# Hybrid decoder layer on Trainium2: a gate projection moved in front of the SSD scan's decay steps, and the sample group's SSD step rearranged

## The reference, cut to what matters

```
def step(h, inp):                       # one chunk
    xi, dti, dai, bi, ci = inp
    cum = jnp.cumsum(dai, axis=1)
    seg = cum[:, :, None] - cum[:, None, :]
    decay = jnp.exp(jnp.where(mask, seg, -jnp.inf))
    cb = jnp.einsum('bign,bjgn->bijg', ci, bi)
    m = cb[..., None] * decay * dti[:, None]
    y = jnp.einsum('bijgh,bjghp->bighp', m, xi)
    y = y + jnp.einsum('bign,bghpn->bighp', ci, h) * jnp.exp(cum)[..., None]
    last = cum[:, -1]
    w = jnp.exp(last[:, None] - cum) * dti
    h = jnp.exp(last)[..., None, None] * h + jnp.einsum('bjgh,bjghp,bjgn->bghpn', w, xi, bi)
    return h, y
...
y = y + ssd_d[:, None] * sx
y = grouped_rmsnorm(y * silu(sz), W['ssd_norm'], SSD_GROUPS)
b_ssd = y @ W['w_ssd_out']
gates = sigmoid(gate_logits)            # three gates of 1024 columns, from the input projection
merged = gates[:, :, 0] * b_lru + gates[:, :, 1] * b_gla + gates[:, :, 2] * b_ssd
```

## Time and profile before

| quantity | value |
|---|---|
| median of 3 runs | 2981.01 us (2977.65 to 2981.55) |
| the profiled execution, its own time | 2984.09 us |
| its span, first to last instruction | 2982.1 us |
| mean granted TensorE clock, as a share of full speed | 0.982 |
| PE busy | 2852.4 us, 96% |
| DVE, ACT, POOL busy | 50%, 24%, 36% |

### The profile page before, as it was taken

How to read it: one execution, slowest core, us unless ns; L and a number is a source line. 1 busy time by engine, 2 the same in 40 slices (tenths; PEclk the granted TensorE clock), 3 DMA queues, 4 the chain that set the end, 5 groups by cost and what they waited for, 6 DMA issues and landing times.

```text
span 2982.1 us, 43536 instructions
## 1 busy us (share of the span) xinstructions
PE 2852.4 (96%) x18264; PEld 2672.6 (90%) x18264; DVE 1480.0 (50%) x2081; ACT 704.9 (24%) x1277; POOL 1077.5 (36%) x729
## 2 busy tenths in 40 slices
PE   7999999999999999989997999899999999999998
PEld 7998999797888899987765999887889999999998
DVE  7886002323342247517852310315368776776665
ACT  4454001123121112215532211204221000001002
POOL 4332322121312223224422343310247888883221
PEclk9999999999999999999998999999999999999999
DMA  4111222212121533231232434134221222225222
GB/s 121 36 43 39 66 65 63 69 34 75 42 68 35 174 125 88 66 103 59 85 98 93 133 101 113 53 102 160 65 88 58 80 66 87 78 71 197 94 89 75
DMA packets 308866, 250.44 MB, mean 84 GB/s; under 512 B 31547, under 2 KB 280444, under 8 KB 308673
## 3 DMA queue, kind: packets, MB, share of 16 engines
q1 hardware_dynamic: 230976, 153.38, 17.6%
q10 hardware_dynamic: 77696, 94.28, 9.5%
HBM read 190.19 MB, written 57.44 MB: 83 GB/s over the span
## 4 chain that ended last, share of the span: by engine, by line
PE 84%; DVE 8%; ACT 3%; DMA 2%; issue 2%; ACTq 0%; POOL 0%; SPq 0%; DVEq 0%
PE PS L937 35%; PE PS L1622 14%; PE PS L1638 8%; PE PS L971 6%; PE PS L1027 3%; DVE WK L2520 3%; PE PS L1035 2%; PE PS L1013 1%; PE PS L1351 1%; PE PS L1327 1%; PE PS L1494 1%; PE PS L1050 1%; PE PS L995 1%; PE PS L1518 1%; PE PM L1195 1%
## 5 line engine op out<-in xcount | busy, mean ns | idle before, releaser
L850 POOL CAST Wh<-Wr 128x1024 fp32r<-128x1024 f32 x169 | 195.0, 1154 | 1570.8 <-DMA Wr<-in_w_in 791.7
L937 PE MATMUL PS<-Hh,Wh 128*128 128x384 f32 (+1 forms) x1904 | 628.2, 330 | 13.5 <-DVE YA L2737 6.3
L937 PE MATMUL PS<-Hh,Wl 128*128 128x384 f32 (+1 forms) x1904 | 622.4, 327 | 0.0
L937 PE MATMUL PS<-Hl,Wh 128*128 128x384 f32 (+1 forms) x1904 | 622.2, 327 | 0.0
L852 POOL TENSOR_TENSOR Wl<-Wr,Wh 128x1024 fp32r<-128x1024 f32 x169 | 435.3, 2576 | 13.5
L937 PEld LDWEIGHTS PS<-Hh,Wh 128*128 128x128 f32 x1904 | 359.0, 189 | 17.2 <-issue 12.5
L937 PEld LDWEIGHTS PS<-Hl,Wh 128*128 128x128 f32 x1904 | 359.1, 189 | 0.6
L937 PEld LDWEIGHTS PS<-Hh,Wl 128*128 128x128 f32 x1904 | 358.9, 188 | 0.0
L2520 DVE SCALAR_TENSOR_TENSOR WK<-WK,PS 128x384 f32<-128x384 f32 (+1 forms) x120 | 63.3, 532 | 444.1 <-PE PS L937 278.9
L3152 DVE TENSOR_TENSOR X<-X,PS 128x384 f32<-128x384 f32 (+1 forms) x264 | 136.3, 531 | 143.0 <-PE PS L1638 79.8
L937 PE MATMUL PS<-Yh,Wh 128*128 128x384 f32 (+1 forms) x576 | 189.5, 329 | 4.8 <-DVE Yl L2690 4.8
(11 more groups left out here) (501 smaller groups left out, 5623.6 us busy)
## 6 DMA issues: line engine op xcount, KB each, us to landing
Wr<-in_w_in SPq DMA_DIRECT2D x82, 512.0 KB, 3.9
X<-f_scr SPq DMA_DIRECT2D x11, 1088.0 KB, 5.0
Wr<-in_w_ffn_gate SPq DMA_DIRECT2D x22, 512.0 KB, 3.8
Wr<-in_w_ffn_up SPq DMA_DIRECT2D x22, 512.0 KB, 4.3
Wr<-in_w_ffn_down SPq DMA_DIRECT2D x22, 512.0 KB, 3.8
merged<-WK ACTq DMA_DIRECT2D x16, 544.0 KB, 4.1
WK<-gates ACTq DMA_DIRECT2D x16, 544.0 KB, 5.0
WK<-merged ACTq DMA_DIRECT2D x16, 544.0 KB, 6.2
```

The source lines that it names most:

```text
L850: pool.tensor_copy(Wh[:, n % SLOTS], Wr[:, n % SLOTS]).then_inc(w_hi, 1)
L937: mm = pe.matmul(bank(f"{name}:{g}")[:, 0:n], L[:, w % SLOTS, k, :], R[:, k, t0:t0 + n], start=(k == 0 and i == 0), stop=(last and k == DT ...
```

## The change

It does the following:

- One whole gate tile (72 steps, three groups, in ring banks 0, 1 and 2) goes between `sums(0)` and `decays(0)`. The gaps behind sequences 2 and 5 are empty (12 steps fewer each), and the two last gaps have 24 steps instead of 48. ACT copies the three groups out behind the exponentials of half chunks 0 and 1.
- `decays(16)` and `matrices(16)` of the samples stand in the scan (behind q = 14), `decays(17)` and `matrices(17)` in the first sequence, `products(16)` and `products(17)` in the last sequence between its last L1409 and its `uc`.
- `turn_state(0)` and `po` stand ahead of `turn_y(15)`; the loads of the first two states are issued one half chunk earlier, and the last prompt output `hi_y(15)` follows the copies of state 0 and `po` on ACT.
- DVE takes the states' part of the outputs straight from both PM banks; the copies through `YI` are gone.
- The samples' two output transposes use one PM bank each (`y_bank`), so the second waits for nothing that the first left.
- On ACT the copies of the gate groups of gap (s, NB) stand behind both `roots_y` of the samples, and the load of z for q = 17 waits for one store less.

```diff
-OWN_BANK |= {"po": 4, f"ss{2 * TT}:0": 3, f"ss{2 * TT + 1}:0": 4, f"sy{2 * TT}:0": 0, f"sy{2 * TT + 1}:0": 1}
-OWN_BANK |= {f"og2_{_t}:{_g}": 5 for _t in range(DT) for _g in range(len(GROUPS))}
+OWN_BANK |= {"po": 4, f"ss{2 * TT}:0": 3, f"ss{2 * TT + 1}:0": 3, f"sy{2 * TT}:0": 0, f"sy{2 * TT + 1}:0": 1}
+OWN_BANK |= {f"og2_{_t}:{_g}": 5 if _t else _g for _t in range(DT) for _g in range(len(GROUPS))}
...
-GAPS |= gap_parts(2, range(DT), [(("q", _q, _i), 12) for _q in range(2 * TT) for _i in range(2)]
-                  + [(("s", _b), 12) for _b in range(NB)] + [(("s", NB), 48), (("s", NB + 1), 48)])
+GAPS |= gap_parts(2, range(DT), [(("q", -1, 0), 72)] + [(("q", _q, _i), 12) for _q in range(2 * TT) for _i in range(2)]
+                  + [(("s", _b), 0 if _b in (2, 5) else 12) for _b in range(NB)]
+                  + [(("s", NB), 24), (("s", NB + 1), 24)])
...
+        def y_bank(q):
+
+            return 1 if q < 2 * TT else q % 2
...
             sums(0)
+            fill(("q", -1, 0))
             decays(0)
             decays(1)
...
-            turn_y(2 * TT - 1)
-
-            read(pe, f"sy{2 * TT - 1}:2")
...
             turn_state(0)
+            read(pe, f"sy{2 * TT - 1}:2")
...
+            turn_y(2 * TT - 1)
+            decays(2 * TT + 1)
             for b in range(NB):
...
                 mm.then_inc(S("si_mm"), 1)
+                if b == NB - 1:
+                    products(2 * TT)
+                    products(2 * TT + 1)
                 name = f"uc{b}"
...
             q = 2 * TT
-            pe.wait_ge(S("act_step"), STEP["yi"])
-            decays(q)
-            decays(q + 1)
-            products(q)
-            products(q + 1)
             fill(("s", NB))
             turn_y(q)
             turn_y(q + 1)
...
-            act.wait_ge(S("si_mm"), NB)
-            act.activation(YI[0][0:TS], PM[0:TS, 0, :], ACT.Copy)
-            act.activation(YI[1][0:TS], PM[0:TS, 1, :], ACT.Copy).then_inc(S("act_step"), 1)
             q = 2 * TT
-            exp_decays(q)
-            exp_decays(q + 1)
-            copy_gates_by_group(("s", NB))
-            for i in range(2):
-                act.wait_ge(S(f"h_put{i}"), 32 * 4)
+            act.wait_ge(S("h_put0"), 32 * 4)
             load_z(q + 1)
+            ready(act, f"sy{q + 1}:0")
             roots_y(q)
             roots_y(q + 1)
+            copy_gates_by_group(("s", NB))
+            act.wait_ge(S("h_put1"), 32 * 4)
             hi_y(q)
             hi_y(q + 1)
...
             dve.wait_ge(S("si_mm"), NB)
-            decay_steps(q + 1)
-            matrices(q + 1)
-            dve.wait_ge(S("act_step"), STEP["yi"])
+
+            y_state = [mark(dve.tensor_tensor(heads(wk(0, 512, 512 * g)[0:TS]), heads(PM[0:TS, g, :]),
+                                              bc(EC(TT)[0:TS, 8 * g:8 * g + 8], HD), MUL)) for g in range(2)]
             outputs(q)
+            outputs(q + 1)
             scale_y(q)
-            outputs(q + 1)
             scale_y(q + 1)
```

More of the change, by code:

```diff
@@ L221, in plan @@
         gap(("q", q, 0))
-        if q + 2 < 2 * TT:
-            banks(f"ss{q + 2}", 2)
+        if q + 2 <= 2 * TT:
+            banks(f"ss{q + 2}", 2 if q + 2 < 2 * TT else 1)
         gap(("q", q, 1))
-    jobs.extend(["po", "si0"])
+    jobs.extend(["si0", "po", f"ss{2 * TT + 1}:0"])
+    q = 2 * TT
     for b in range(NB):
-        jobs.extend([f"ub{b}"] + ([f"si{b + 1}"] if b + 1 < NB else []) + [f"uc{b}"])
+        jobs.extend([f"ub{b}"] + ([f"si{b + 1}"] if b + 1 < NB else [f"sy{q}:0", f"sy{q + 1}:0"]) + [f"uc{b}"])
         gap(("s", b))
-    q = 2 * TT
-    banks(f"ss{q}", 1)
-    banks(f"ss{q + 1}", 1)
-    banks(f"sy{q}", 1)
-    banks(f"sy{q + 1}", 1)
     for i in range(2):
@@ L298 @@
 STEP = {name: n + 1 for n, name in enumerate(("eps", "sc", "nb", "dt_raw", "dt_done", "h_zero", "dab", "cz"))}
-STEP |= {name: n + 1 for n, name in enumerate(("lam_exp", "dt_exp", "yi", "mem_std"))}
+STEP |= {name: n + 1 for n, name in enumerate(("lam_exp", "dt_exp", "mem_std"))}
 FIRST_W = {}
@@ L896, in _ @@
             weight_x(q, "skip")
-            pool.wait_ge(S("si_mm"), NB)
-            read(pool, f"ub{NB - 1}")
+            pool.wait_ge(S("y_std"), 2 * TT)
             weight_x(q + 1, "skip")
@@ L1372, in _ @@
                 fill(("q", q, 0))
-                if q + 2 < 2 * TT:
+                if q + 2 <= 2 * TT:
                     decays(q + 2)
                 fill(("q", q, 1))
-            turn_y(2 * TT - 1)
-            read(pe, f"sy{2 * TT - 1}:2")
-            free_bank(pe, "po")
-            for k in range(4):
-                mm = turn(bank("po")[:, k * P:(k + 1) * P], H_ssd[:, k * P:(k + 1) * P], P)
-            done(mm, "po")
-            pe.wait_ge(S("dve_step"), STEP["cz"])
-            pe.wait_ge(S("sc_exp"), TT + 1)
-            pe.wait_ge(S("cbm"), TT + 1)
-            pe.wait_ge(S("sy_lo"), 2 * TT)
-            pe.wait_ge(S("wx2"), 2)
             def turn_state(b):
@@ L1396, in _ @@
             turn_state(0)
+            read(pe, f"sy{2 * TT - 1}:2")
+            free_bank(pe, "po")
+            for k in range(4):
+                mm = turn(bank("po")[:, k * P:(k + 1) * P], H_ssd[:, k * P:(k + 1) * P], P)
+            done(mm, "po")
+            turn_y(2 * TT - 1)
+            decays(2 * TT + 1)
             for b in range(NB):
@@ L1407, in _ @@
                 read(pe, f"si{b}")
+                if b == 0:
+                    pe.wait_ge(S("dve_step"), STEP["cz"])
+                    pe.wait_ge(S("sc_exp"), TT + 1)
+                    pe.wait_ge(S("cbm"), TT + 1)
+                    pe.wait_ge(S("sy_lo"), 2 * TT)
                 for g in range(2):
@@ L2177, in hi_y @@
                 for k in range(4):
[L2178 removed]
+                    ins = act.activation(Yh[:, 4 * g + k, c * P:c * P + n], PM[:, y_bank(q), k * P:k * P + n], ACT.Copy,
                                          scale=PV[:, 4 * g + k, R_NSSD:R_NSSD + 1])
@@ L2190, in _ @@
                     exp_sums(q // 2 + 1)
+                if q == 2 * TT - 1:
+                    for b in range(2):
+                        state_in(b)
                 if q:
@@ L2199, in _ @@
                 copy_gates_by_group(("q", q, 1))
-            for b in range(2):
-                state_in(b)
-            hi_y(2 * TT - 1)
-            ready(act, "po")
-            freed(act.activation(wk(2, 512), bank("po"), ACT.Copy), "po")
-            read(act, "po")
-            n_stores[0] += 2
-            state_out(O["p_ssd_h"][0, 0], wk(2, 512), stored)
-            SO = [wk(6, 512, 512), wk(4, 512, 512)]
+            SO = [wk(4, 512, 512), wk(6, 512, 512)]
             def copy_state(b):
@@ L2218, in copy_state @@
                 freed(act.activation(wk(1, 512, b % 2 * 512), bank(name), ACT.Copy), name)
-            act.wait_ge(stored, 16 * n_stores[0])
-            act.wait_ge(S("dve_step"), STEP["cz"])
             for b in range(NB + 1):
+                if b == 0:
+                    ready(act, f"sy{2 * TT - 1}:1")
                 if b < NB:
                     copy_state(b)
+                if b == 0:
+                    ready(act, "po")
+                    freed(act.activation(SO[1], bank("po"), ACT.Copy), "po")
+                    read(act, "po")
+                    n_stores[0] += 2
+                    state_out(O["p_ssd_h"][0, 0], SO[1], stored)
+                    hi_y(2 * TT - 1)
+                    exp_decays(2 * TT + 1)
                 if b:
@@ L2226, in _ @@
                     ready(act, name)
+                    if b == 1:
+                        act.wait_ge(S("y_turned"), 2 * TT)
+                    if b == 2:
+                        act.wait_ge(stored, 16 * n_stores[0])
                     if b >= 3:
@@ L2981, in _ @@
                 scale_y(q)
-            split_y(2 * TT - 1)
             dve.tensor_tensor(CZ, mid(wk(1)[:, LP:T], NB), seqm[:], MUL).then_inc(S("dve_step"), 1)
-            decay_steps(2 * TT)
+            ready(dve, "po")
+            decay_steps(2 * TT + 1)
             for b in range(NB):
@@ L2991, in _ @@
                     .then_inc(S("bm"), 1)
+                if b == 0:
+                    split_y(2 * TT - 1)
                 read(dve, f"si{b}")
```

30 lines of the change are left out of this document (16 added, 14 removed).

## The result

The changed kernel takes 2950.0 us (median of 4 runs, 2946.78 to 2955.15) where the kernel before, run beside it, takes 2979.33 us (4 runs, 2973.45 to 2981.55). The ratio is 0.9897, 95% interval 0.9879 to 0.9915: faster by 29 us. The profiled execution took 2955.15 us around a span of 2953.2 us; the mean clock is 0.982 in both traces.

The account below looks back on a forecast made before the run. PE, busy for 96% of the span, bounds the kernel; only its waits and half speed can be saved. Terms 3.3 + 0.9 - 2.6 - 4.0 - 26.0 = -28.4 us, against the 2981.01 median 2952.6 us; range 2942 to 2965.

Parts of the forecast that it names:

- Start: Start of the scan: moved tile, decays, sums(1), products(0), two bank waits of 0.7, 1.5 for a spell; +3.3 us.
- Loop: The scan's loop: decays(16) comes in, while projection steps cover the added DVE and ACT instructions; +0.9 us.
- Middle: End of the scan to the first sequence's fill: 15.2 us becomes 12.6, with 2.8 for lower clock; -2.6 us.
- Sequences: The sequences: 2 and 5 lose 12 steps each and nothing new waits; -4.0 us.
- Tail: After the sequences, up to ob2_0: 47.5 us becomes 21.5, with 3.9 for half speed; -26.0 us.
- Behind the stage: After the SSD stage: PE's wait of 5.7 us for the memory's transposes stays, so no change.
- Rival 1: Whole stage: the clock holds and all three half-speed allowances fall away; -36.6 us, 2944.4 us; chance 0.15.
- Rival 2: First sequence or end: late chain longer, PE waits 5 to 8 us more; about -17 us, 2964; chance 0.12.
- rival 3: Start of the scan: PE waits with the tile, hole unfilled; start +12, sum -20 us, 2961; chance 0.06.
- rival 4: Sequences: lower clock spreads, eight rounds of about 8.5 us add 27; sum +15.4 us, 2996; chance 0.04.

Follow-up runs that it names:

- mats_late: The changed kernel with the samples' decays, exponentials, matrices and products put back behind the last sequence; 2955.69 us, ratio 0.9913 to the kernel before.
- hi_first: The changed kernel with hi_y(15) on ACT ahead of the copies of state 0 and po; 2942.35 us, ratio 0.9872 to the kernel before.
- hi_z_root: The changed kernel with hi_y(15) first, z's load ahead of the last uc, and the memory's root ahead of the gates' tanh on ACT; 2933.29 us, ratio 0.985.
- act_old: The changed kernel with ACT's old order at the end: gate copies, both store waits, then z's load and the roots; 2953.53 us, ratio 0.9914.
- z_early: The changed kernel with the load of z for q = 17 issued ahead of ACT's wait for the last uc; 2944.47 us, ratio 0.9894.

## Why the prediction was right

It said 2952.6 us, 2942 to 2965, by the filled hole and the shortened chain behind the sequences; 2950.0 was measured. The two large steps, the filled hole and the shortened tail, happened as said. That the sums agree within 1 us (-28.4 and -29.2 in the stage) is partly luck: the profile has a spell worth about 5 us that most others lack, and without it the stage is 34.0 us shorter than before. By its own steps:

- **Start, +3.3, measured +3.6: right in size, partly by luck.** In 9 of 12 profiles of kernels with the tile the start takes 21.8 or 21.9 us, with no spell; that is the 22.6 of the prediction with bank waits of 0.32 and 0.26 us instead of two of 0.7. Three profiles, the changed kernel's own among them, have a spell of about 10 us from 1353.9 us on (granted clock 0.50), 5.6 us of it before the loop, and so 24.4. The 1.5 us allowed for a spell stand between the two cases, 0 and 2.8.
- **Loop, +0.9, measured +0.8,** by luck, with the same spell's rest in it (2.3 us, where the loop before has a spell worth 1.7). Without a spell the loop takes 166.5 to 167.5 us with `decays(16)` and 165.4 without it (mats_late), so the term itself was about right, and the moved DVE and ACT work was mostly hidden.
- **Middle, -2.6, measured -3.4.** Its waits were turn_y 0.94 (said 1.0), L1328 1.39 (0.8), L1413 1.00 (1.9), `uc0` 1.44 (1.4). hi_first shows that the order on ACT behind L1413's wait was rightly named: it goes when `hi_y(15)` goes first.
- **Sequences, -4.0, measured -2.2: the term that was mis-sized.** The steps did leave; but the half speed that the middle caused lasted into them, to 1545.1 us, 3.6 us more than before, worth 1.8. State 0's 12 steps took 4.1 us, not 2.0. I had charged the middle for its sparse work, and let the spell end with it. hi_z_root, whose sequences ran at 1.00, has 31.5 there, 4.4 less than before, about what 24 steps cost.
- **Tail, -26.0, measured -27.9.** `products(16)` and `(17)` took 2.0 us, not 3.6 (0.058 us from one record to the next; a half chunk has 8 matmuls with two records each, and the "16 matmuls" in the list ahead of the prediction are records): the 1.9 each of the earlier trace rows had been taken at half speed, which the row doesn't say and the stretch's clock of 0.75 does. z went out at 6.7, not 8.4; the waits were 1.85 and 0.74 (said 1.5, and 0.5 by its own times); half speed cost 3.4 (3.9). act_old and z_early both show that z's load is what the tail hangs on: later by 4.0 us costs 3.0, earlier by 7.4 gives 4.8.
- **Behind the stage, 0, measured -2.3.** PE's wait for the memory did not stay: it fell from 5.7 to 4.6 us, mostly because the scalings took 1.42 us instead of 2.19. They took up to 4.3 us, and the wait up to 8.8, in other kernels. The rest goes with a half-speed spell behind it, which lasts 3.4 us instead of 6.8; why it is shorter stays open. The prediction had no term for POOL's split beside DVE; that it did little harm here is luck.
- **Rivals.** Rival 1 (the clock holds) was wrong for the changed kernel, 27 us of its stage are at half speed against 51 before, but right in part for the start; it becomes nearly true in hi_z_root, whose stage has 3.4 us at half speed. Rival 2's long waits, rival 3's unfilled hole and rival 4's eight slow rounds did not come. Of the two readings in the Trainium skill's page "TensorE: Matmul & The Clock Gate", the trace agrees with the section on short idling between groups ("A second HAM failure mode: psum-queue depth-cycling"): after the middle's waits of 1.0 to 1.4 us PE was at half speed up to 1545.1, and in z_early, where the tail's waits shrank to 0.5 us, the level stayed up to `ob2_0`.

What the runs settle about the parts: the two large ones are the tile with its table (about 12 us) and the chain behind the sequences (ACT's order and z), the main part of the 19 to 22 us of the rearrangement; the early matrices give 2 us at most, the direct read of PSUM nothing, the second bank nothing that one profile shows.

## What to carry to other kernels

A hole in which the bottleneck engine waits is worth filling with independent work even when the last stretch seems the natural place for it; but the load or chain that ends the next stretch then has to be moved ahead too, and its successor after it, each found as the new longest wait. Ask of each duration at which clock it was measured before it enters a sum, and of two profiles whether both have the same spells before their stretches are subtracted. A half-speed spell can outlast the sparse stretch ahead of it, as it did here by 4.9 us. An engine's queue with DMA issues in it is ordered by who waits for what it issues, not by the order in which the data come.
